# Key, query and value projections ahead of the spatial ones, the linear attention beside 48 weight tiles, the spatial gate inside it in a PSUM bank of its own

## The chip, the cores and the metric

The kernel runs on one core of one Trainium2 chip. The metric is the device time of one execution in microseconds (us); lower is better. TensorE is called PE below, VectorE DVE, ScalarE ACT, GpSimdE POOL, and SyncE SP.

## What is computed

Two transformer blocks in a row, on 256 tokens of width 1024, in fp32. The change touches the token mixer of the second block only. Cut to that:

```python
z = h @ w_in                                   # 8 parts: u vs q r ga gb k v, and lr (32 columns)
u, vs, q, r, ga, gb, k, v, lr = split(z)
vn = layer_norm(gelu(vs), sgu_ln_g, sgu_ln_b)
s  = einsum('gpq,bnqgc->bnpgc', sgu_w, vn) + sgu_b      # spatial gate
a  = gelu(u) * s
la = log_sigmoid(lr @ w2 + b2) / 16            # log decays, two directions
o  = gla_forward(q, k, v, la_f, s0f) + gla_backward(q, k, v, la_b, s0b)   # chunks of 64 tokens
ob = o * rsqrt(mean(o*o) + eps) * gla_norm_g * silu(r)
x  = x + g1 * ((sigmoid(ga) * (a @ w_br_a) + sigmoid(gb) * (ob @ w_br_b)) @ w_o)
```

`s0f` and `s0b`, the initial states, come from the same recurrence over a second input, the context (`ctx`), for which k, v and lr alone are projected. With the mean and variance of the layer norm taken per token, the gain `sgu_ln_g` and the shift `sgu_ln_b` are per column of `vs`.

## The kernel before

Every weight tile ("slot") is 128 x 1024 numbers and comes by its own DMA into one of six raw buffers. ACT rounds it to `w_hi` (`fill` in `act_program`, L776), DVE subtracts to `w_lo` (`fill` in `dve_program`, L1235), both in rings of four, and PE multiplies with three fp32r matmuls for each product: `tall` (L318 to L320, 24 matmuls over 256 tokens, one output chunk of 128 columns) or `wide` (12 matmuls over 512 columns). While PE works on slot s, the slots s+1 to s+3 can be ready; the `fill` of slot s+4 waits until PE has used slot s, since it overwrites its buffer.

The order is written out by hand, and each engine runs its own list strictly in order. For a stage of n slots, ACT does for each slot: evacuate the product (`evac`), `fill` for slot s+4, and one step of a side task; DVE does `fill` for s+4 and one step of its side task; PE does the slot and one step of its side task. A side task is a generator (`Side`), each `yield` of which ends a step. So step k stands behind slot k of the stage on every engine, and behind the fill that waits for PE's slot k on ACT and DVE. `claim(bank)` on PE waits until whoever reads a PSUM bank has released it; the releaser stands in `emptied`.

The product of slot n goes to bank n % 4 (`RING`), banks 0 to 3; the side tasks use banks 4 to 7. `project_tokens` uses banks (0, 1) and then (2, 3) for four slots each.

The stages of the second block's mixer before, with their side tasks:

- `u` (8 slots), `vs0`, `vs1` (4 wide slots each), beside `context_states`: log decays of the context, their scans, the decayed keys (the product with the keys on POOL, L1889), PE transposes, initial states.
- `lr`, `k`, `q`, `v0`, `v1` (17 slots), beside `spatial_gating`: gelu of `vs` and `u`, the norm (its gain and shift on POOL, L1905 and L1907), eight small PE products in four pairs, one pair for each of banks 4 to 7, then bias and gate on DVE (L1552, L1557, L1560).
- `r`, `ga`, `gb`, `br_a` (32 slots), beside `linear_attention`: log decays, scans, decayed keys (POOL), scores, three steps of the state in halves, the outputs (`gla_o`), the head norms (`sum`, `power`), `r_scaled` on POOL, `ob` and `ob_low`.
- `br_b`, `w_o2`, and the feed-forward part.

In `log_decays` before, DVE adds the bias (L1487), takes minus the absolute value (L1493), ACT takes exp and ln (L956, L958), and DVE combines (L1498).

Of the kernel before, what the change touches and what calls it, by code (L numbers as in the profile page):

```python
# [7 lines left out]
P = 128  # L8
D = 1024
# [33 lines left out]
          ("u", KC), ("vs0", 4), ("vs1", 4), ("lr", 1), ("k", 4), ("q", 4), ("v0", 4), ("v1", 4),  # L43
# [26 lines left out]

def raw_of(kind, n):
    return LOAD_OF[kind, n] % RAW
# [10 lines left out]
def down_slot(l, j):  # L83
# [5 lines left out]
             ("gla_b2", 2 * GH), ("gla_g", 8), ("fconv", 9 * FC), ("fconv_b", FC)]  # L89
VEC_AT, VEC_N = {}, 0  # L90
for _name, _n in VEC_PARTS:
# [7 lines left out]
    "decay_act": ("decay_exp", "decay_ln", "kd_exp", "q_exp", "k_exp", "dec"),  # L99
    "conv_act": ("img", "conv_mid", "conv_first"),  # L100
    "gates_act": ("sig_a", "sig_r", "sig_b", "vs_gelu", "u_gelu"),
    "memory_dve": ("ma_max0", "ma_max", "ma_rc", "ma_prob", "ma_lo"),
    "stick_dve": ("z_kept", "minus_log_not", "log_not_first", "log_not", "log_a", "am_part", "am"),
    "decay_dve": ("decay_b", "decay_abs", "decay", "scan", "decay_left"),
# [6 lines left out]
    "spatial_dve": ("sg_bias", "sg_gated", "sg_lo"),  # L111
    "vs_normed": ("vn_scaled", "vn"),
# [4 lines left out]
class Signals:  # L117
# [56 lines left out]
def build(nc, table, stream, vec, xT, memT, ctxT, c_rows, sq_consts, masks, scan_mask, sgu_bc, sgu_wT, gla_w2, out):  # L174
    pe, act, dve, pool, sp = nc.tensor, nc.scalar, nc.vector, nc.gpsimd, nc.sync
    with ExitStack() as ctx:
# [26 lines left out]
        LR = sb("LR", [P, T])  # L203
# [34 lines left out]
        BC, WS = area(20736, 3, D), area(23808, KC, P)  # L238
        UB, VSB = area(0, KC, T), area(2048, TT, D)
        RB, GA, GB = area(4096, KC, T), area(6144, KC, T), area(8192, KC, T)  # L240
        KB, QB, VB = area(10240, GH, T), area(11264, GH, T), area(12288, TT, D)
        QD = area(14336, 2, GH, T)
        KI, KD = area(0, 2, GH, T), area(2048, 2, GH, T)
        CKI, CKD = area(6144, 2, GH, T), area(8192, 2, GH, T)
        ST = [area(at, 2 * GH, 256) for at in (16384, 18432, 0, 10240)]
# [62 lines left out]
        def pe_program():  # L308
# [46 lines left out]
            def project(stage, count, h, release, side=None, ready=None, steps=1):  # L355
                assert n == AT[stage], (stage, n)
                for i in range(count):
                    b = n % RING
# [174 lines left out]
            def log_decays(s):  # L533
                for d in range(2):
                    claim(4 + 2 * d, 5 + 2 * d)
                    pe.wait_ge(*past("lr", s))
                    for hh in range(GH):
                        last = mm(PS[:, 4 + 2 * d + hh // 2, (hh % 2) * T:(hh % 2 + 1) * T],
                                  W2[32 * d:32 * d + RANK, hh * P:(hh + 1) * P],
                                  LR[32 * d:32 * d + RANK, :], hh % 2 == 0, True)  # L540
                    last.then_inc(*mark("decay_z", s, d))
                    emptied[4 + 2 * d] = emptied[5 + 2 * d] = [("decay_b", s, d, GH - 1)]
                    yield
                yield from nothing(4)

            def transpose_kd(s, kd):
                pe.wait_ge(*past("kd", s, 1))
                for d in range(2):
# [26 lines left out]
            def spatial_gating():  # L575
# [3 lines left out]
                for c in range(KC):  # L579
                    b = 4 + c // 2  # L580
                    if c % 2 == 0:
                        claim(b)
# [3 lines left out]
                    if c % 2 == 0:  # L586
                        continue
# [1465 lines left out]
```

## Time and profile before

| | us |
|---|---|
| median of the timed runs (3) | 1255.36 (1255.06 to 1255.45) |
| profiled execution, its own time | 1260.26 |
| its span, first to last instruction | 1258.9 |
| PE busy (matmul) | 1177.7, 94% |
| DVE busy | 846.1, 67% |
| ACT busy | 626.4, 50% |
| POOL busy | 218.8, 17% |
| mean granted clock of PE | 0.975 of full |

PE is busy for nearly the whole span, so what is won or lost is the time in which it stands still or runs at the lower clock. All positions below are us from the start of the span. The stages that the change touches lie between 718.68, PE's first matmul of `u`, and 994.24, its first of `br_b`; `w_o2` starts at 1019.49.

### The profile page before, as it was taken

How to read it: one execution, taken by the hardware profiler on the slowest of the kernel's cores; microseconds unless marked ns; L12 is line 12 of the kernel's file. 1: busy time of each engine (PE TensorE's matmuls, PEld its weight loads, DVE VectorE, ACT ScalarE, POOL GpSimd, SP SyncE). 2: the span in 40 equal slices, each digit the busy share in tenths (PEclk: the TensorE clock that was granted, in tenths of full speed). 3: DMA queues.
4: the chain of work that ended last, by engine and by line, in shares of the span. 5: the costliest groups of instructions: out<-in, count | busy, mean ns of one | idle time of the engine just before them, and what ended most of it. 6: DMA issues, size and time to landing. Idle time of an engine off the chain costs nothing.

```text
span 1258.9 us, 21745 instructions
## 1 busy us (share of the span) xinstructions
PE 1177.7 (94%) x8974; PEld 1132.0 (90%) x8974; DVE 846.1 (67%) x1234; ACT 626.4 (50%) x942; POOL 218.8 (17%) x156
## 2 busy tenths in 40 slices
PE   6999999999889799999999998999799897999996
PEld 5989999999888689999999887889789797999996
DVE  4577677778764656777787664766663576777775
ACT  5645534435555545444446545544721545555553
POOL 2002100001210012000000001300100112565562
PEclk9999999999989799999999999999899898999999
DMA  7545687776543045778876444454342263546540
GB/s 290 171 158 183 192 277 250 242 239 228 198 159 122 12 186 180 247 242 269 268 251 215 157 131 148 138 163 134 118 128 84 75 194 108 181 164 192 190 162 34
DMA packets 60321, 222.91 MB, mean 177 GB/s; under 512 B 6736, under 2 KB 6992, under 8 KB 59584
## 3 DMA queue, kind: packets, MB, share of 16 engines
q1 hardware_dynamic: 59760, 219.05, 53.2%
q10 hardware_dynamic: 288, 2.10, 0.4%
q8 instruction: 71, 1.16, 0.4%
q0 software_dynamic: 176, 0.39, 0.1%
q14 instruction: 26, 0.21, 0.1%
HBM read 220.46 MB, written 1.05 MB: 176 GB/s over the span
## 4 chain that ended last, share of the span: by engine, by line
PE 76%; DVE 12%; ACT 6%; issue 3%; POOL 2%; DMA 1%; SPq 0%; ACTq 0%; DVEq 0%; POOLq 0%
PE PS L318 21%; PE PS L320 21%; PE PS L319 21%; PE PS L323 13%; DVE w_lo L1235 4%; ACT w_hi L776 3%; DMA X<-xT 1%; DVE SQ L1271 1%; DVE ARENA L1755 1%; DVE SQ L1509 1%; ACT ARENA L858 1%; POOL ARENA L1905 1%; DVE ARENA L1271 1%; POOL ARENA L1907 0%; DVE raw L1257 0%
## 5 line engine op out<-in xcount | busy, mean ns | idle before, releaser
L1235 DVE TENSOR_TENSOR w_lo<-raw,w_hi 128x1024 fp32r<-128x1024 f32 x325 | 410.3, 1265 | 276.2 <-ACT w_hi L776 275.7
L776 ACT ACTIVATE w_hi<-raw 128x1024 fp32r<-128x1024 f32 x356 | 372.1, 1053 | 156.3 <-PE PS L320 131.8
L318 PE MATMUL PS<-Y_hi,w_hi 128*128 128x256 f32 x1240 | 360.7, 291 | 20.7 <-DVE Y_lo L1633 5.9
L319 PE MATMUL PS<-Y_lo,w_hi 128*128 128x256 f32 x1240 | 355.0, 286 | 0.0
L320 PE MATMUL PS<-Y_hi,w_lo 128*128 128x256 f32 x1240 | 354.9, 286 | 0.0
L318 PEld LDWEIGHTS PS<-Y_hi,w_hi 128*128 128x128 f32 x1240 | 242.2, 195 | 28.6 <-issue 17.4
L319 PEld LDWEIGHTS PS<-Y_lo,w_hi 128*128 128x128 f32 x1240 | 242.4, 195 | 0.1
L320 PEld LDWEIGHTS PS<-Y_hi,w_lo 128*128 128x128 f32 x1240 | 242.1, 195 | 0.0
L318 PE MATMUL PS<-H_hi,w_hi 128*128 128x256 f32 x808 | 233.1, 288 | 5.5 <-issue 2.5
L319 PE MATMUL PS<-H_lo,w_hi 128*128 128x256 f32 x808 | 229.1, 284 | 0.0
L320 PE MATMUL PS<-H_hi,w_lo 128*128 128x256 f32 x808 | 229.0, 283 | 0.0
L318 PEld LDWEIGHTS PS<-H_hi,w_hi 128*128 128x128 f32 x808 | 155.5, 192 | 10.6 <-issue 5.8
L319 PEld LDWEIGHTS PS<-H_lo,w_hi 128*128 128x128 f32 x808 | 155.6, 193 | 0.2
L320 PEld LDWEIGHTS PS<-H_hi,w_lo 128*128 128x128 f32 x808 | 155.5, 192 | 0.0
L318 PE MATMUL PS<-G_hi,w_hi 128*128 128x256 f32 x528 | 149.6, 283 | 3.4 <-DVE G_lo L1363 3.4
L319 PE MATMUL PS<-G_lo,w_hi 128*128 128x256 f32 x528 | 149.4, 283 | 0.0
L320 PE MATMUL PS<-G_hi,w_lo 128*128 128x256 f32 x528 | 149.4, 283 | 0.0
L318 PEld LDWEIGHTS PS<-G_hi,w_hi 128*128 128x128 f32 x528 | 101.3, 192 | 3.9 <-DVE w_lo L1235 2.0
L320 PEld LDWEIGHTS PS<-G_hi,w_lo 128*128 128x128 f32 x528 | 101.4, 192 | 0.0
L319 PEld LDWEIGHTS PS<-G_lo,w_hi 128*128 128x128 f32 x528 | 101.4, 192 | 0.0
L1845 POOL TENSOR_TENSOR GF<-GF,RS 128x256 f32<-128x256 f32 x44 | 32.6, 742 | 340.5 <-ACT GF L894 340.5
L894 ACT ACTIVATE GF<-GF 128x256 f32<-128x256 f32 x44 | 18.3, 417 | 145.3 <-DVE GF L1374 145.3
(194 smaller groups left out, 1467.7 us busy)
## 6 DMA issues: line engine op xcount, KB each, us to landing
raw<-stream SPq DMA_DIRECT2D x404, 512.0 KB, 4.0
ARENA<-memT SPq DMA_DIRECT2D x2, 1024.0 KB, 6.0
ARENA<-sgu_bc ACTq DMA_DIRECT2D x1, 1536.0 KB, 11.2
X<-xT SPq DMA_DIRECT2D x1, 1024.0 KB, 11.3
ARENA<-c_rows SPq DMA_DIRECT2D x2, 512.0 KB, 6.9
ARENA<-ctxT SPq DMA_DIRECT2D x1, 1024.0 KB, 7.7
outT<-ARENA SPq DMA_DIRECT2D x2, 512.0 KB, 2.6
CROW<-c_rows SPq DMA_DIRECT2D x1, 512.0 KB, 8.7
```

The source lines that it names most:

```text
L318: pe.matmul(o, wh, xh, start=start, stop=False, skip_group_check=True)
L319: pe.matmul(o, wh, xl, start=False, stop=False, skip_group_check=True)
L320: return pe.matmul(o, wl, xh, start=False, stop=stop, skip_group_check=True)
L323: return pe.matmul(o, w, x, start=start, stop=stop, skip_group_check=True)
L776: act.activation(w_hi[n % RING][:], raw[at][:], ACT.Copy).then_inc(*mark("hi", n))
L858: act.activation(EX[:, i], PS[:, bs[h], t * T:(t + 1) * T], ACT.Exp, bias=nmx[:, i:i + 1], scale=HD ** -0.5, accum_out=sm[:, i:i + 1]).the ...
L894: act.activation(GF[:], GF[:], ACT.Silu).then_inc(*mark("silu", l, j))
L1235: dve.tensor_tensor(w_lo[n % RING][:], raw[raw_of("slot", n)][:], w_hi[n % RING][:], ALU.subtract).then_inc(*mark("lo_dve", n))
L1271: dve.scalar_tensor_tensor(via[:, c], src[:, c], g(c), rs[1], ALU.mult, ALU.mult).then_inc(*mark("norm", tag, c))
L1509: dve.tensor_tensor_scan(dst, first, src, 0.0, ALU.mult, ALU.add).then_inc(*mark("scan", s, d, hh))
L1755: dve.scalar_tensor_tensor(ACC[:, b + 1 - k], IMG[:, r0:r0 + ROWS, c0:c0 + COLS], gain("fconv", j + t * FC), ACC[:, b + 1 - k], ALU.mult, ...
L1845: pool.tensor_tensor(GF[:], GF[:], RS[:, 0], ALU.mult).then_inc(*mark("silu_rs", l, j))
```

## The change

The stages are reordered to `lr`, `k`, `q`, `v0`, `v1` (17 slots, beside `context_states`) and then `u`, `vs0`, `vs1`, `r`, `ga`, `gb`, `br_a` (48 slots, beside one `linear_attention`, in which the spatial gate lies). Steps are now named: `pace.to(k)` makes what follows it part of step k. From stage `r` to `w_o2` the slots use three banks (0 to 2), and bank 3 serves the spatial gate and, as before, the head norms. ACT takes the absolute value straight out of PSUM with the bias added, in four instructions for a direction, and DVE's bias instruction takes the minimum with 0 as well. The decayed keys are made by DVE. The gain and shift of the layer norm leave POOL: the gain is applied behind the product, the shift goes into the bias through two more PE products (`sg_rows`) and eight DVE instructions. Three things of the arithmetic have their own buffers now (two of `KB`, two of `VB`, two halves of `LR`). The DMA of `sgu_bc` shrinks from 1536 KB to 512 KB.

The steps of the parts that the diff below leaves out: in both new side tasks, PE has the log decays in steps 1 and 2; ACT has their absolute values, exp and ln in 2 and 3; DVE has the minimum in 2 and 3, `decay` and the scan of one direction in 4 and 5, of the other in 6 and 7, `decay_left` in 8 and 9, the decayed keys in 10 and 11. Beside the context, DVE has the eight `sg_bias` instructions in step 8, and ACT has `kd_exp` in 9 and 10, the copies of the transposes in 13. In `linear_attention`, ACT has `q_exp` and `k_exp` in 6 and 8, `dec` and `kd_exp` in 9 and 10, the copies of the transposes in 14, the gelu of `vs` in 17, that of `u` and the table of exp in 18, the layer norm's root in 19; DVE has `qd` in 12 and 13, `ki` in 14 and 15, the masked copies of the scores (`sc`) in 17, the statistics of `vs` in 18, `silu_r` in 28 to 31, `ob` in 36 to 39 and `ob_low` in 41 to 44.

```diff
@@ order of the stages, and the banks
-          ("u", KC), ("vs0", 4), ("vs1", 4), ("lr", 1), ("k", 4), ("q", 4), ("v0", 4), ("v1", 4),
+          ("lr", 1), ("k", 4), ("q", 4), ("v0", 4), ("v1", 4), ("u", KC), ("vs0", 4), ("vs1", 4),
+def bank_of(n):
+    return n % 3 if AT["r"] <= n < AT["ffn2"] else n % RING
+class Pace:
+    def __init__(self):
+        self.at = 1
+    def to(self, step):
+        while self.at < step:
+            self.at += 1
+            yield
@@ pe_program, context_states
-                yield from log_decays(0)
-                yield from nothing(7)
-                yield from transpose_kd(0, CKD)
+                yield from log_decays(0, pace)
+                yield from pace.to(6)
+                claim(4, 5)
+                pe.wait_ge(*past("late_in", 1))
+                for half in range(2):
+                    last = mm(PS[:, 4 + half].rearrange("p (c q) -> p c q", c=4), ONES, WS[:, 4 * half:4 * half + 4])
+                last.then_inc(*mark("sg_rows"))
+                emptied[4] = emptied[5] = [("sg_bias", KC - 1)]
+                yield from pace.to(12)
+                transpose_kd(0, CKD)
+                yield from pace.to(15)
...
@@ pe_program, the gate
+            def spatial_gating(pace):
+                for c in range(1, KC, 2):
+                    yield from pace.to(21 + c // 2)
+                    claim(3)
+                    pe.wait_ge(*past("vs_unit", 1))
+                    for k in (c - 1, c):
+                        for t in range(TT):
+                            last = mm(PS[:, 3, (k % 2) * T + t * P:(k % 2) * T + (t + 1) * P],
+                                      VSB[:, t, k * P:(k + 1) * P], WS[:, k], k % 2 == 0 and t == 0, True)
                     last.then_inc(*mark("sg", c // 2))
+                    emptied[3] = [("sg_gated", c // 2)]
@@ pe_program, linear_attention
+                yield from pace.to(13)
+                transpose_kd(1, KD)
+                yield from pace.to(16)
                 pe.wait_ge(*past("ki", 1))
...
+                    if step == GN - 2:
+                        yield from spatial_gating(pace)
+                    for turn in range(2 * GH):
+                        if turn % GH == 0:
+                            yield from pace.to((18, 20, 25)[step] + turn // GH)
+                        hh, d = turn // 2, turn % 2
+                        i = d * GH + hh
...
                 for hh in range(GH):
+                    yield from pace.to(28 + hh)
...
                 for hh in range(GH):
+                    if hh % 2 == 0:
+                        yield from pace.to(33 + hh // 2)
                     if hh % 2 == 0:
                         claim(3)
@@ act_program, log_decays; linear_attention
+                    yield from pace.to(2 + d)
+                    act.wait_ge(*past("decay_z", s, d))
+                    for hh in range(GH):
+                        act.activation(tmp[:, d, hh], PS[:, 4 + 2 * d + hh // 2, (hh % 2) * T:(hh % 2 + 1) * T],
+                                       ACT.Abs, bias=gain("gla_b2", d * GH + hh)).then_inc(*mark("decay_abs", s, d, hh))
...
+            def spatial_gating(pace):
                 for c in range(1, KC, 2):
+                    yield from pace.to(22 + c // 2)
                     act.wait_ge(*past("sg_gated", c // 2))
+                    act.activation(Y2[0][:, c - 1:c + 1], UB[:, c - 1:c + 1],
                                    ACT.Copy).then_inc(*mark("sg_hi", c // 2))
+                yield from pace.to(27)
+                act.wait_ge(*past("r", KC - 1))
+                act.activation(GB, RB, ACT.Sigmoid).then_inc(*mark("sig_r"))
+                exp_set()
+                yield from pace.to(32)
                 act.wait_ge(*past("gla_o", GH - 1))
...
                 for i in range(2):
+                    yield from pace.to(34 + i)
                     power(f"head{i}", RS4[:, 2 * i:2 * i + 2], PS[:, 3].rearrange("p (h t) -> p h t", h=2), 1.0 / 256,
                           ("sum", f"head{i}"))
                 for hh in range(GH):
+                    yield from pace.to(41 + hh)
+                    if hh == 0:
+                        act.wait_ge(*past("gb", KC - 1))
+                        act.activation(GA, GA, ACT.Sigmoid).then_inc(*mark("sig_a"))
+                        act.activation(GB, GB, ACT.Sigmoid).then_inc(*mark("sig_b"))
+                        exp_set()
+                    ob_split(hh)
@@ dve_program
+                yield from pace.to(19)
+                states(0, 0)
+                yield from pace.to(20)
+                states(0, 1)
+                vs_units()
+                yield from pace.to(21)
+                states(1, 0)
                 dve.wait_ge(*past("sc", 1))
                 dve.tensor_tensor(SC[:, 0], SC[:, 0], SC[:, 1], ALU.add).then_inc(*mark("sc_sum"))
+                yield from pace.to(22)
+                states(1, 1)
+                yield from spatial_gating(pace)
+                for half in range(2):
+                    yield from pace.to(26 + half)
+                    states(2, half)
@@ dve_program, the gate
+            def spatial_gating(pace):
                 for c in range(1, KC, 2):
+                    yield from pace.to(22 + c // 2)
+                    two = slice(c - 1, c + 1)
                     dve.wait_ge(*past("sg", c // 2))
                     for k in range(2):
+                        v = PS[:, 3, k * T:(k + 1) * T].rearrange("p (t q) -> p t q", t=TT)
+                        dve.scalar_tensor_tensor(v, v, gain("sgu_g", c - 1 + k),
+                                                 SB[:, c - 1 + k].unsqueeze(1).to_broadcast([P, TT, P]), ALU.mult,
+                                                 ALU.add).then_inc(*mark("sg_scaled", c // 2, k))
+                    dve.wait_ge(*past("sg_scaled", c // 2, 1))
                     dve.wait_ge(*past("u_gelu", 1))
+                    dve.tensor_tensor(UB[:, two], PS[:, 3].rearrange("p (c t) -> p c t", c=2), UB[:, two],
                                       ALU.mult).then_inc(*mark("sg_gated", c // 2))
                     dve.wait_ge(*past("sg_hi", c // 2))
+                    dve.tensor_tensor(Y2[1][:, two], UB[:, two], Y2[0][:, two],
                                       ALU.subtract).then_inc(*mark("sg_lo", c // 2))
```

## Rows read from the trace of the kernel before

**Rows 1.** The page, busy time of each engine over the span

```profile
PE 1177.7 (94%) x8974; PEld 1132.0 (90%) x8974; DVE 846.1 (67%) x1234; ACT 626.4 (50%) x942; POOL 218.8 (17%) x156
```

**Rows 2.** Windows, three side tasks, `br_b`: us, PE, PEld, DVE, ACT, POOL busy, PE clock, DMA

```profile
718.68:782.14 63.46, 58.57 (x353) 51.48 (x352) 37.47 (x39) 31.00 (x37) 4.75 (x2) 1.00 0.47 151
782.14:839.59 57.45, 53.81 (x347) 48.80 (x345) 37.90 (x36) 30.52 (x40) 12.53 (x4) 0.97 0.42 138
839.59:946.20 106.61, 99.16 (x712) 93.32 (x712) 70.69 (x89) 51.53 (x69) 4.74 (x2) 0.95 0.41 129
946.20:1019.49 73.29, 67.17 (x537) 65.99 (x537) 36.07 (x56) 28.55 (x34) 5.40 (x4) 0.95 0.32 101
```

**Rows 3.** Windows from slot start to slot start: slots alone, then with side products

```profile
852.53:864.05 11.52, 11.52 (x98) 11.52 (x97) 4.72 (x4) 6.40 (x8) 0.00 (x0) 1.00 0.34 112
750.27:758.43 8.16, 8.16 (x38) 6.76 (x37) 8.16 (x12) 1.06 (x1) 0.00 (x0) 1.00 0.50 170
721.64:726.63 4.99, 4.99 (x34) 4.34 (x33) 3.26 (x6) 1.33 (x2) 0.00 (x0) 1.00 0.57 167
828.34:834.69 6.35, 6.35 (x34) 5.40 (x33) 5.35 (x8) 2.65 (x3) 0.00 (x0) 1.00 0.37 112
898.75:902.50 3.75, 3.75 (x35) 3.75 (x34) 3.75 (x4) 3.53 (x4) 0.00 (x0) 1.00 0.45 144
...
963.85:971.19 7.34, 7.34 (x66) 7.34 (x65) 1.65 (x2) 1.06 (x1) 0.00 (x0) 1.00 0.24 74
772.61:782.14 9.53, 9.53 (x47) 8.25 (x46) 2.45 (x2) 4.44 (x5) 0.00 (x0) 1.00 0.74 249
```

**Rows 4.** Timeline of PE: start, duration, line, and its idle time before, with releaser

```profile
813.91 1.71 PE L323 MATMUL PS<-ARENA 128*128 128x128 f32 x8 [2.01 <-POOL ARENA L1907]
...
839.59 0.39 PE L318 MATMUL PS<-Y_hi,w_hi 128*128 128x256 f32 x1 [1.11 <-ACT ARENA L844]
...
884.40 0.36 PE L318 MATMUL PS<-Y_hi,w_hi 128*128 128x256 f32 x1 [2.73 <-DVE w_lo L1235]
...
890.28 0.55 PE L318 MATMUL PS<-Y_hi,w_hi 128*128 128x256 f32 x1 [2.77 <-DVE w_lo L1235]
...
917.91 1.96 PE L323 MATMUL PS<-ARENA,SQ 64*128 64x256 f32 x8 [1.08 <-DVE ARENA L1595]
...
994.24 0.55 PE L318 MATMUL PS<-Y_hi,w_hi 128*128 128x256 f32 x1 [5.87 <-DVE Y_lo L1633]
```

**Rows 5.** Timeline of ACT behind the slot that ended at 929.34

```profile
929.45 0.38 ACT L833 ACTIVATE ARENA<-PS 128x256 f32<-128x256 f32 x1 [3.65 <-PE PS L320]
929.73 1.05 ACT L776 ACTIVATE w_hi<-raw 128x1024 fp32r<-128x1024 f32 x1
```

**Rows 6.** Timeline of DVE behind the same slot, and in the gate before

```profile
821.77 0.75 DVE L1552 TENSOR_TENSOR SQ<-PS,ARENA 128x256 f32<-128x256 f32 x2
822.55 0.69 DVE L1557 TENSOR_TENSOR SQ<-SQ,ARENA 128x512 f32<-128x512 f32 x1
...
916.45 1.32 DVE L1595 COPY_PREDICATED ARENA<-mask_sb,PS 128x1024 f32<-128x1024 uint32 x1
...
930.81 1.23 DVE L1235 TENSOR_TENSOR w_lo<-raw,w_hi 128x1024 fp32r<-128x1024 f32 x1 [2.19 <-ACT w_hi L776]
931.95 1.65 DVE L1611 SCALAR_TENSOR_TENSOR ARENA<-ARENA,small,PS 128x256 f32<-128x256 f32 x4
```

**Rows 7.** Timeline of ACT in the first head norm, and a table load

```profile
983.82 0.69 ACT L787 ACTIVATE ARENA<-PS,EPS_COL 128x512 f32<-128x512 f32 x1 [1.10 <-PE PS L323]
984.54 0.63 ACT L789 ACTIVATE ARENA<-ARENA 128x512 f32<-128x512 f32 x1
...
997.07 1.28 ACT L1178 ACT_TABLE_LOAD   x1
```

**Rows 8.** Windows behind the wait ahead of `br_b`, and at 890.28

```profile
994.24:998.60 4.36, 4.36 (x19) 4.09 (x20) 3.51 (x6) 2.78 (x4) 1.00 (x1) 0.50 0.02 4
...
890.28:895.54 5.26, 5.26 (x25) 5.26 (x26) 2.70 (x3) 4.97 (x7) 0.00 (x0) 0.50 0.64 199
```

More of the change, by code:

```diff
@@ L110 @@
     "modulation": ("mod_dot", "mod"),
[L111 to L112 removed]
+    "spatial_dve": ("sg_bias", "sg_scaled", "sg_gated", "sg_lo"),
 }
@@ L1510, in scans, with decayed_keys @@
                                                ALU.add).then_inc(*mark("scan", s, d, hh))
-                    yield
+            def decayed_keys(s, d, kd):
+                dve.wait_ge(*past("kd_exp", s, d))
+                dve.wait_ge(*past("kb", s, GH - 1))
+                dve.tensor_tensor(kd[:, d], kd[:, d], KB[s], ALU.mult).then_inc(*mark("kd", s, d))
             def context_states():
+                pace = Pace()
                 dve.wait_ge(*past("norm_hi", "norm1", KC - 1))
-                yield from log_decays(0, CKI)
-                yield from scans(0, CKI, ONES[:, 0:1].to_broadcast([P, T]))
+                yield from log_decays(0, CKI, pace)
+                yield from pace.to(8)
+                dve.wait_ge(*past("sg_rows"))
+                dve.wait_ge(*past("late_in", 1))
+                for c in range(KC):
+                    dve.scalar_tensor_tensor(SB[:, c], PS[:, 4 + c // 4, (c % 4) * P:(c % 4 + 1) * P], gain("sgu_b", c),
+                                             SB[:, c], ALU.mult, ALU.add).then_inc(*mark("sg_bias", c))
                 for d in range(2):
+                    yield from pace.to(8 + d)
                     e = 0 if d else T - 1
@@ L1624, in linear_attention @@
                                       ALU.mult).then_inc(*mark("ob", hh))
-                    if hh:
-                        ob_low(hh - 1)
-                    yield
-                ob_low(GH - 1)
+                for hh in range(GH):
+                    yield from pace.to(41 + hh)
+                    ob_low(hh)
             def ob_low(hh):
@@ L1711, in dve_program @@
             side = Side(linear_attention())
-            beside(16, side)
-            dve.wait_ge(*past("sig_r"))
-            for c in range(KC):
-                dve.scalar_tensor_tensor(RB[:, c], RB[:, c], gain("gla_g", c), GB[:, c], ALU.mult,
-                                         ALU.mult).then_inc(*mark("silu_r", c))
-            beside(KC, side)
+            beside(5 * KC, side)
             def branch_a(i, s):
@@ L1925, in pool_program @@
             side = Side(linear_attention())
-            fills(4 * KC, side)
+            fills(6 * KC, side)
             side.finish()
```

379 lines of the change are left out of this document (138 added, 241 removed).

## The prediction

> **What bounds the kernel now.** I read the page first: PE is busy 1177.7 us of a span of 1258.9 [rows 1], so only time in which PE stands or runs slowly can move, and work that PE gains or loses. Then windows over the stages, set against what PE has to do in them. A tall slot takes 2.88 us (11.52 for four), a wide one 2.72 (8.16 for three). The side products cost, beyond their slots, 2.11 for a log decay (4.99 - 2.88), 0.91 for a pair of gate products (6.35 - 2 x 2.72), 0.87 for eight transposes (3.75 - 2.88), 4.46 for a `gla_o` (7.34 - 2.88), 6.8 for all context states (9.53 - 2.72) [rows 3]. A half step of the state has the four products of a log decay (2.1), a `scores` twice a gate pair (1.8), a head sum is put at 2.0. From 718.68 to 1019.49 PE has 57 tall slots (164.2), 16 wide (43.5), 4 log decays (8.4), 4 sets of transposes (3.5), the context states (6.8), 4 gate pairs (3.6), 2 scores (3.6), 6 halves (12.6), 4 `gla_o` (17.8), 2 sums (4.0): 268.0. The windows add up to 300.8 [rows 2]. So 32.8 us are loss: 6.0, 6.1, 12.5 and 8.3 in the four windows. This is all that the change can win there. The larger waits show whence it comes: the gain and shift of the norm on POOL (2.01, then a slot at the low clock), two late `w_lo` (2.73 and 2.77, ACT having stood in its queue for `decay_left`), the masked scores (1.08), and 5.87 at `br_b` for the last `Y_lo` [rows 4]. Behind the last one PE runs 4.36 us at half the granted clock, 1.2 GHz; behind the pair, 5.26 [rows 8].
>
> **The change, part by part.** The slots, log decays, transposes, states and outputs are the same in number; only order and side steps differ. So I sum what PE loses in the new order and set it against 32.8. An engine's step k stands behind its fill, and that waits for PE's slot k. The delay of this is in the rows: the slot ended at 929.34, ACT evacuated at 929.45 and filled from 929.73, DVE filled from 930.81, and its step began at 931.95: 2.6 us after the slot [rows 5, 6]. That number decides most of what follows.
>
> 1. New PE work, `sg_rows`: two fp32 products of 512 columns. The context states are 16 of 256 columns in 6.8, so 0.43 each, and this is four times that: +1.8 (1.5 to 2.2).
> 2. Turns of banks, where the next slot needs the bank just filled. Behind a pair of wide banks ACT copies for 1.0 us, and PE idles 1.11 and restarts slowly, 1.4 in all [rows 4]; this falls due at `u`. At `v0` a 0.38 copy does it, 0.7. At `vs0` the same copy comes behind `q_exp` and `k_exp`, 1.1 (0.7 to 1.5). The turn at `r` is hidden by the scores, 3.6. Sum 3.2.
> 3. Context keys: DVE makes `kd` of the second direction in step 11, two steps of DVE work ending about 3.6 behind PE's slot 11, while PE asks after 2.72 + 0.87. With the backlog of the scans and of eight `sg_bias`, each between 0.25 and 0.41 (a 256 column one: 1.65 for four [rows 6]), I take 0.7 (0 to 1.7).
> 4. `ki` of step 15: behind the copies of the transposes ACT fills late, DVE's fill and `ki` end 6.8 after slot 14, and PE asks after two wide slots, 5.4: 1.4 (0.5 to 2).
> 5. Scores: DVE copies two masks of 1.2 each from 2.6 after slot 17, ready at 5.1, and PE wants the second bank at 3.3: 1.75. The trace had 1.08 here [rows 4].
> 6. The gate. PE's four pairs stand in steps 21 to 24, all in bank 3, and each claims the bank from DVE's gating of the one before. But DVE does that in steps 22 to 24, behind the fill for the very slot that PE has just ended. So PE's pair in step 23 waits 2.6 for DVE's step to begin, two scalings (0.9; the two bias instructions took 0.75), the product (0.69 [rows 6]), 0.1 for the signal: 4.3. Step 24 the same. In step 22 DVE has first half a step of the state, four instructions for 1.6 [rows 6]: 5.9. Nothing is left for PE in that time: its next slot stands behind the pair in its own queue, and behind PE's wait ACT and DVE get no used buffer. Sum 14.5. Before, four pairs had four banks and never waited for a gate. Bounds: 12.5 if scalings from PSUM to PSUM are as quick as the bias and restarts are free, 16 if they take 0.2 more.
> 7. The last half of the state stands in DVE's step 27 and PE wants it after slot 28, with no side product between: 2.6 + 1.6 + 0.1 - 2.88 = 1.5.
> 8. Squares of the output: ACT's evacuation comes first now, 0.5.
> 9. Head norms: PE's second sum (step 34) claims bank 3 from ACT's first `power`, moved to step 34 as well: evacuation and fill 1.4, then 0.69 and 0.63 [rows 7]: 2.85. Before, it was in the step of the sum, and hidden.
> 10. `sig_a` and `sig_b` stand together on ACT in step 41: two table loads of 1.28 [rows 7] and two sigmoids of 2048 columns at 1.9 (a fill of 1024 takes 1.05 [rows 5]), 6.3 us; `ob_hi` follows, DVE waits for it ahead of the evacuation of the second `br_a`, and the third slot from there wants its bank of three: 0.8. The 5.87 at `br_b` is gone, since `ob_low` ends four slots ahead.
> 11. Clock. After 5.87 of standing PE ran 4.36 at 1.2 GHz [rows 8], 2.2 lost. Three waits of 4 to 6 us with 3.8 of work between: 2.0 each (1.2 to 2.7), 6.0. For the smaller waits around the scores and head norms 1.5 (0 to 4).
> 12. First tiles of wide stages, 0.3.
>
> The decay chain that cost ga its two waits I put at nothing: its scans are now two steps apart, ACT waits for each alone, about 2 us by the 2.6 above, and three ready slots of weights, 8.6 us, cover that; without this cover it costs up to the old 2.73 + 2.77 and their clock, 8. POOL's products on DVE take a `w_lo`'s 1.23 each [rows 6], which fits beside the fill into a slot's 2.88. The shorter DMA is put at nothing: PE waits for a DMA only at the very start.
>
> Sum: 1.8 + 3.2 + 0.7 + 1.4 + 1.75 + 14.5 + 1.5 + 0.5 + 2.85 + 0.8 + 7.5 + 0.3 = 36.8 against 32.8, +4.0. On the profiled 1260.26 (span 1258.9 and 1.4 around it) this is 1264.3. That execution is 4.9 above the median of the runs; taken over to it: 1255.36 + 4.0 = 1259.4.
>
> **The rivals.** *A, the clock hardly falls.* The first of the two waits for `w_lo`, 2.73, left the clock alone: PE's next matmul took 0.36, the one behind the second 0.55 [rows 4]. If the gates cost 1.2 each and the smaller waits nothing, the sum is 3.9 less: 1255.5, no change. Against it: each gate's wait is over 4 us.
>
> *B, the gates are free.* This holds if DVE gates before PE asks, that is if its step is not bound to the slot, or if the 2.6 are shorter than the pair. Then items 6 and the 6.0 of clock fall away: 1238.9, faster. For it speaks only that the gate before never stood; but it had four banks and two slots to each pair. It decides at a chain of under about 1 us behind the slot, and the rows have 4.3.
>
> *C, the clock stays down.* Once it is low, the three slots, three pairs and the half step behind them run at 1.2 GHz throughout: 8.6 + 2.7 + 2.1 = 13.4 instead of 6.0, which gives 1266.8. The rows for it: the low clock outlasted a whole slot at 890.28 [rows 8], after two waits of 2.7 with a single slot between, the very pattern of the gates. The Trainium skill (TensorE: Matmul & The Clock Gate, A second HAM failure mode: psum-queue depth-cycling) speaks against the change here: a kernel whose matmul groups take turns in PSUM banks pauses so often between them that the clock keeps falling and rising. By that rule C would be the case; the trace agrees for two waits, not beyond.
>
> *D, the old chain comes back.* DVE has the decayed keys, the eight `sg_bias` and the minimum now; if its backlog reaches 6 us in one of the decay chains, `w_lo` is late again, up to 8 more. It would land in C's place, near 1266.
>
> **How the numbers follow.** The forecast has 0.60, A 0.13, B 0.10, C and D together 0.17. The forecast's own range, with the bounds above taken by half, is 1256 to 1262.5. For 8 in 10, A and most of C come in: 1253.5 to 1266. This kernel's measurement tells 0.2% (2.5 us) from no change, so same is 1252.9 to 1257.9. Faster: B and a little of A, 0.12. Same: most of A and the lower edge of the forecast, 0.25. Slower: 0.63.
>
> **What would show it.** PE rows of the gate (four products of 128 columns, bank 3) behind idle times of nearly 5.9, 4.3, 4.3, released by DVE's gating, and a granted clock of a half around them; an idle time of 2.8 ahead of the second head sum, released by ACT's exp; none of more than 1 ahead of `br_b`; the two 2.7 waits for `w_lo` gone; POOL idle from the first block to the head norms. If the waits ahead of the gate are under 1 us, item 6 is wrong and with it the forecast. If they stand but the time is lower, the clock or an item of 2 to 5 is over-priced.

## The result, and the profile after

| | before | after |
|---|---|---|
| median of the timed runs (5 each, taken together) | 1255.45 (1255.06 to 1256.67) | 1263.15 (1261.01 to 1264.79) |
| profiled execution, its own time | 1260.26 | 1264.79 |
| its span | 1258.9 | 1263.5 |
| mean granted clock | 0.975 | 0.974 |

The ratio after to before is 1.0044, 95% interval 1.0033 to 1.0055: on 1255.4 that is 5.5 us slower (4.1 to 6.9). The two medians are 7.7 apart, the two profiled executions 4.5. The five runs after spread over 3.8 us, the 29 runs of the kernel before that were timed beside e1 to e4 over 7.6, and the times go with the granted clock: of the five runs after, the two at 0.979 took 1261, the three at 0.974 to 0.976 took 1263 to 1265. So below, single waits are compared in the traces and totals in the medians. One run of e4, of 1640.72 us at a granted clock of 0.648, is left out of everything below.

The page after, busy time of each engine, answers to [rows 1]:

```profile
PE 1178.6 (93%) x8978; PEld 1132.7 (90%) x8978; DVE 840.2 (66%) x1242; ACT 632.4 (50%) x958; POOL 195.4 (15%) x148
```

Windows of the kernel after, in the columns of [rows 2]: the context's side task; `linear_attention` up to and with the scores; from there up to and with the first gate pair; the slots and pairs of the gate; the rest to `w_o2`; and what follows:

```profile
718.75:783.94 65.19, 62.98 (x382) 55.29 (x380) 36.88 (x47) 34.80 (x47) 0.00 (x0) 1.00 0.45 147
783.94:841.12 57.18, 54.91 (x353) 49.26 (x353) 41.08 (x44) 37.09 (x50) 0.00 (x0) 1.00 0.46 147
841.12:864.30 23.18, 21.36 (x164) 18.83 (x162) 15.41 (x23) 13.38 (x18) 0.00 (x0) 1.00 0.35 115
864.30:901.00 36.70, 22.54 (x125) 21.79 (x123) 14.84 (x25) 5.87 (x9) 0.00 (x0) 0.72 0.18 58
901.00:1021.72 120.72, 115.53 (x937) 113.05 (x937) 63.14 (x89) 56.55 (x72) 7.04 (x4) 0.99 0.41 131
1021.72:1263.50 241.78, 224.45 (x1796) 221.43 (x1794) 173.42 (x283) 126.57 (x208) 115.42 (x60) 0.97 0.45 149
```

The stretch of the last one in the kernel before:

```profile
1019.49:1258.90 239.41, 222.11 (x1796) 219.37 (x1794) 168.68 (x283) 126.55 (x208) 118.40 (x60) 0.98 0.46 150
```

The stages of the change now take 302.97 us, from 718.75 to 1021.72, where they took 300.81. The fourth window is the change's own: 36.70 us, of which PE works 22.5, at a mean clock of 0.72. None of the other four up to `w_o2` has a clock below 0.99. The waits of PE in these stages (us in total, times, the longest), without two smaller ones of 0.5 and 0.3; all together are 25.8:

```profile
PE PS L339 <- DVE ARENA L1572: 14.2, 3, 5.8
PE PS L339 <- ACT ARENA L808: 2.7, 1, 2.7
PE PS L339 <- ACT ARENA L852: 1.9, 2, 1.3
PE PS L339 <- DVE ARENA L1621: 1.5, 2, 1.0
PE PS L339 <- DVE ARENA L1586: 1.5, 1, 1.5
PE PS L334 <- ACT ARENA L863: 1.1, 1, 1.1
PE PS L339 <- DVE ARENA L1614: 0.9, 1, 0.9
PE PS L334 <- DVE ARENA L1741: 0.6, 1, 0.6
PE PS L567 <- DVE ARENA L1519: 0.6, 1, 0.6
```

L1572 is the gate's product on DVE, L808 the exp of a head norm, L852 and L863 the copies out of the banks, L1621 the masked scores, L1586 the states, L1614 `ki`, L1741 the evacuation of `br_a`, L1519 the decayed keys. The old waits for `w_lo` and the 5.87 for `Y_lo` [rows 4] are gone; which part of the change took each away, no run tests. PE's timeline at the gate (start, duration, idle time before, releaser), and DVE's behind the slot in between:

```profile
873.18 2.08 PE L339 MATMUL PS<-ARENA 128*128 128x128 f32 x8 [5.76 <-DVE ARENA L1572]
884.14 2.08 PE L339 MATMUL PS<-ARENA 128*128 128x128 f32 x8 [4.20 <-DVE ARENA L1572]
894.77 2.08 PE L339 MATMUL PS<-ARENA 128*128 128x128 f32 x8 [4.20 <-DVE ARENA L1572]
```

```profile
868.81 1.22 DVE L1244 TENSOR_TENSOR w_lo<-raw,w_hi 128x1024 fp32r<-128x1024 f32 x1 [1.46 <-ACT w_hi L795]
869.95 1.65 DVE L1586 SCALAR_TENSOR_TENSOR ARENA<-ARENA,small,PS 128x256 f32<-128x256 f32 x4
871.52 0.88 DVE L1567 SCALAR_TENSOR_TENSOR PS<-PS,V,ARENA 128x256 f32<-128x256 f32 x2
872.43 0.69 DVE L1572 TENSOR_TENSOR ARENA<-PS,ARENA 128x512 f32<-128x512 f32 x1
...
881.34 1.23 DVE L1244 TENSOR_TENSOR w_lo<-raw,w_hi 128x1024 fp32r<-128x1024 f32 x1 [6.83 <-ACT w_hi L795]
882.48 0.88 DVE L1567 SCALAR_TENSOR_TENSOR PS<-PS,V,ARENA 128x256 f32<-128x256 f32 x2
883.39 0.69 DVE L1572 TENSOR_TENSOR ARENA<-PS,ARENA 128x512 f32<-128x512 f32 x1
```

The granted clock behind the first of these waits, over the pair and over 3.47 us of the slot behind it (us, PE busy, clock, DMA share, GB/s, as in all windows of PE alone below):

```profile
873.18:874.91 1.73, 1.73 (x9) 0.50 0.00 0
874.91:878.38 3.47, 3.47 (x18) 0.50 0.00 0
```

The chain can be read off row by row: the slot ends, ACT and DVE fill, DVE's step begins (half a state first, in one case), two scalings, the product, and only then PE starts its pair. DVE, whom all wait for, stands 6.83 itself, for a fill that waits for PE.

### The profile page after: what moved, and what is told of

The parts are those of the page before. It is cut to its first block, busy times and chain, and to the rows that moved or that the text cites. A ratio compares the mean times of both kernels' runs of the same rounds, so it can differ in the third digit from the quotient of the medians.

```text
span 1263.5 us, 21778 instructions
## 1 busy us (share of the span) xinstructions
PE 1178.6 (93%) x8978; PEld 1132.7 (90%) x8978; DVE 840.2 (66%) x1242; ACT 632.4 (50%) x958; POOL 195.4 (15%) x148
## 4 chain that ended last, share of the span: by engine, by line
PE 78%; DVE 11%; ACT 6%; issue 4%; DMA 1%; SPq 0%; POOL 0%; ACTq 0%; DVEq 0%
PE PS L334 22%; PE PS L335 21%; PE PS L336 21%; PE PS L339 14%; DVE w_lo L1244 3%; ACT w_hi L795 3%; DVE ARENA L1774 1%; DMA X<-xT 1%; DVE SQ L1280 1%; ACT ARENA L877 1%; DVE ARENA L1280 1%; DVE raw L1266 0%; DVE ARENA L1586 0%; PE PS L428 0%; DVE ARENA L1427 0%
## 5 line engine op out<-in xcount | busy, mean ns | idle before, releaser
L1244 DVE TENSOR_TENSOR w_lo<-raw,w_hi 128x1024 fp32r<-128x1024 f32 x325 | 405.6, 1249 | 316.1 <-ACT w_hi L795 315.6
L852 ACT ACTIVATE ARENA<-PS 128x256 f32<-128x256 f32 x70 | 26.7, 382 | 120.1 <-PE PS L336 119.9
```

Source lines behind the costliest of these rows:

```text
L852: act.activation(dst[:, i], PS[:, bank_of(s), 0:T], ACT.Copy).then_inc(*mark(name, *index, i))
L1244: dve.tensor_tensor(w_lo[n % RING][:], raw[raw_of("slot", n)][:], w_hi[n % RING][:], ALU.subtract).then_inc(*mark("lo_dve", n))
```

## The experiments

None of them changes what is computed. They were timed in later rounds than the kernel after, each set beside runs of the kernel before, whose median was 1256.12 for e1 to e4, 1256.84 for e5 to e8 and 1258.10 for e9 and e10, where it had been 1255.45. So a difference of two medians holds up to 2.7 us of drift between rounds. The table therefore has, beside the medians, the difference of the two ratios to the kernel before, taken times 1255.4 ("by ratios"); its error is 2 to 3 us. Since the scatter of the clock reaches into the totals, a second measure is used, taken in each profile: the distance from PE's `sg_rows` to its norm sum behind `w_o2`, which frames all that differs between these kernels. In the kernel after, the two rows are:

```profile
740.24 1.88 PE L339 MATMUL PS<-ARENA,consts 128*128 128x512 f32 x4
...
1046.84 0.67 PE L339 MATMUL PS<-SQ,consts 128*128 128x256 f32 x2 [1.92 <-POOL SQ L1849]
```

This is 306.60 us. The table has the same distance for the others, read from the same two rows.

| kernel | median (runs) | ratio to before, 95% | against after, by ratios | distance | against after, distance |
|---|---|---|---|---|---|
| after | 1263.15 (5) | 1.0044, 1.0033 to 1.0055 | | 306.60 | |
| e1 gate spaced | 1255.16 (12) | 0.9992, 0.9980 to 1.0005 | -6.5 | 298.42 | -8.2 |
| e2 order in the half step | 1261.59 (6) | 1.0049, 1.0036 to 1.0063 | +0.6 | 303.85 | -2.8 |
| e3 PE kept busy | 1256.22 (12) | 1.0009, 0.9992 to 1.0026 | -4.4 | 297.59 | -9.0 |
| e4 head norm's step | 1256.44 (11) | 1.0010, 0.9999 to 1.0020 | -4.3 | 299.21 | -7.4 |
| e5 one direction | 1269.92 (6) | 1.0099, 1.0080 to 1.0119 | +6.9 | 314.19 | +7.6 |
| e6 gate in the same step | 1248.64 (6) | 0.9934, 0.9914 to 0.9954 | -13.8 | 294.14 | -12.5 |
| e7 banks exchanged | 1261.07 (9) | 1.0031, 1.0021 to 1.0042 | -1.6 | 303.80 | -2.8 |
| e8 combined | 1230.54 (4) | 0.9796, 0.9779 to 0.9813 | -31.1 | 273.49 | -33.1 |
| e9 before, directions mixed | 1254.96 (12) | 0.9978, 0.9967 to 0.9990 | | | |
| e10 combined, outputs later | 1227.08 (4) | 0.9751, 0.9734 to 0.9767 | -36.8 | 271.05 | -35.6 |

### e1: two slots to each gate pair

```diff
-                    yield from pace.to(21 + c // 2)        # PE
+                    yield from pace.to(21 + 2 * (c // 2))
-                    yield from pace.to(22 + c // 2)        # ACT, DVE
+                    yield from pace.to(22 + 2 * (c // 2))
```

and what follows the gate, three steps later. With it, ACT's sigmoid of `r` comes ahead of its last part of the gate, and DVE's last half states stand among its steps for `silu_r`.

> The changed kernel with PE's four gate pairs in steps 21, 23, 25, 27 and the gating of DVE and ACT in 22, 24, 26, 28, still in bank 3 alone; the last state, the outputs and the head norms move back by three steps. Theory G (the gate's claim of bank 3 is bound to DVE's step of the same number): the three idle times of 5.8, 4.2, 4.2 ahead of the gate vanish, and with them some 8 us of half clock; 1241, 22 us under the changed kernel. Rival R (sharing one bank is itself the loss, or the time comes back later): the waits shrink but others grow; less than 8 us are won.

```profile
873.01 1.16 PE L339 MATMUL PS<-ARENA 128*128 128x128 f32 x8 [2.89 <-DVE ARENA L1573]
881.24 1.16 PE L339 MATMUL PS<-ARENA 128*128 128x128 f32 x8 [1.32 <-DVE ARENA L1573]
889.47 1.16 PE L339 MATMUL PS<-ARENA 128*128 128x128 f32 x8 [1.32 <-DVE ARENA L1573]
...
908.47 7.78 PE L339 MATMUL PS<-ARENA 128*128 128x128 f32 x39 [3.82 <-DVE ARENA L1587]
```

The waits are not gone, they are 2.87 and 2.88 shorter: exactly one slot. The expectation had them gone altogether. But DVE still gates in the step behind PE's pair, that step is itself bound to a slot's end, and the spacing only gives PE a second slot to work on meanwhile. And a new wait of 3.82 stands ahead of the outputs, where the last half states now come behind a fill that came late and behind `silu_r`. At the gate itself the clock stays full (1.00 from 864.12 to 893.43), as the theory had it. But behind the 3.82 it falls: the first output and the slot after it take 12.16 us at a clock of 0.58, where they take 7.41 in the kernel after. So 1255.2 and not 1241: 8.0 us are won by the medians, 6.5 by the ratios, the size that rival R gave. The miss says that distance alone, by one slot, is the poorer remedy.

### e6: the gate's DVE part in PE's own step

```diff
-                    yield from pace.to(22 + c // 2)        # ACT, DVE
+                    yield from pace.to(21 + c // 2)
```

and the half states of steps 21 and 22 behind the gates.

> The changed kernel with DVE's and ACT's part of each gate in the very step of PE's pair (21 to 24 instead of 22 to 25), the state halves of step 1 behind the gates; the pairs stay in consecutive steps and in the one bank 3. Theory S (the gate waits come from the step in which DVE stands, one slot behind PE's pair, and not from the bank being one): the chain behind a slot is 2.6 + 0.9 + 0.7 + 0.1 = 4.3, and PE asks after the pair and the next slot, 3.8: waits of 0.5, growing to at most 2 as the two state halves (1.6 each) are put on DVE between the gates; 14.2 of waits become 2 to 4 and most of the 7 us of clock goes too: 1243 to 1249. Rival B (one bank for four pairs costs its 4 us whatever the step): waits and time stay, 1263. Rival W (DVE's added load in these steps makes a w_lo late): gate waits small, but a wait for w_lo of 2 to 4 around step 24 to 26, 1250 to 1254.

```profile
869.52 1.05 PE L339 MATMUL PS<-ARENA 128*128 128x128 f32 x8
875.26 1.61 PE L339 MATMUL PS<-ARENA 128*128 128x128 f32 x8 [1.82 <-DVE ARENA L1572]
880.87 1.16 PE L339 MATMUL PS<-ARENA 128*128 128x128 f32 x8
```

The pairs are as close together as after, and all in bank 3; still 12.4 of the 14.2 are gone, and the time is 14.5 us less by the medians, 13.8 by the ratios. From the first pair to the half step behind the last slot, 37.55 us became 19.14. This is theory S: with the same single bank, 1.8 of waiting is left, and in e8 none. What costs is that DVE's answer stands one step behind PE's question, so that DVE begins it only when PE, its slot done, already asks for the bank again. The clock gained nothing on balance in this profile: the 6.0 us won at the gate beyond the waits were lost in two stretches at half clock elsewhere, 3.0 and 3.2; the windows from the scores' wait on, ahead of all that the edit touches, and in the outputs:

```profile
848.55:855.71 7.16, 7.16 (x31) 0.53 0.23 76
...
897.49:908.06 10.57, 10.57 (x64) 0.68 0.24 84
```

### e3: the same waits, PE kept busy in them

```diff
...
                     yield from pace.to(21 + c // 2)
+                    if c > 1:
+                        busy_work(36 if c == 3 else 24)   # products into the next slot's bank, overwritten by it
                     claim(3)
...
```

`busy_work` itself claims that bank and waits for the next slot's weights first.

> The changed kernel with idle work on PE ahead of the second, third and fourth claim of the gate: 36, 24 and 24 extra products of the next slot's weights (results are overwritten), about 4.3, 2.9 and 2.9 us, which end before the bank comes free. Theory C (about 8 of the gate's 22 us are the half clock behind its waits): the clock stays at full, the slots behind take 2.9 to 3.1 again, 8 us faster, 1255. Rival (the clock costs nothing beyond the waits): within 1 us of the changed kernel.

Idle times of 1.45, 1.32 and 1.32 are left, and the window over the gate has PE at full clock throughout:

```profile
864.39:893.68 29.29, 25.19 (x207) 1.00 0.22 72
```

In the kernel after, the same stretch:

```profile
864.30:900.96 36.66, 22.50 (x123) 0.72 0.18 58
```

36.66 less 29.29 is 7.4, with the chains of DVE unchanged: that is what the low clock costs at the gate, on top of 14.2 of standing. The distance fell by 9.0, as one more stretch of low clock is missing: the second head sum waits 2.66, as after, but it and the slot behind it then take 4.70 us at a clock of 1.00, against 6.36 at 0.73. Useless work on PE brings 6.9 us by the medians, 4.4 by the ratios, and two of the twelve runs, at 1263.25 and 1264.37, gained nothing. So the clock's part at the gate is shown in the trace; how much of it reaches the total is known only to 2 or 3 us.

### e4: the head norm's power in the step of its sum

```diff
-                    yield from pace.to(34 + i)
+                    yield from pace.to(33 + i)
                     power(f"head{i}", RS4[:, 2 * i:2 * i + 2], ...
```

> The changed kernel with ACT's roots of the head norms in steps 33 and 34 instead of 34 and 35. Theory H: the idle 2.65 us ahead of the second head sum goes, and with it a stretch of half clock that falls due behind it; 2.7 to 4 us faster, 1259.5 to 1260.5. Rival: ACT then waits for the sum ahead of its next fill and a slot comes late; no gain.

```profile
943.23 1.96 PE L339 MATMUL PS<-SQ,consts 128*128 128x256 f32 x8 [0.46 <-ACT SQ L1054]
947.90 1.89 PE L339 MATMUL PS<-SQ,consts 128*128 128x256 f32 x8
```

The 2.65 are gone. The distance fell by 7.4, more than the edit can give. In the kernel after, the slot ahead of the second sum (with the wait), the sum itself and the slot behind it took 3.0, 1.4 and 0.5 more than they must, the last two at a clock that had fallen; 4.6 of this is gone. The median is 6.7 lower, 4.3 by the ratios. The other 2.8 fell in the gate, which the edit does not touch (see e2).

### e2: another order within the half step

```diff
-                        hh, d = turn // 2, turn % 2
+                        hh, d = 2 * (turn // GH) + turn % 2, turn // 2 % 2
```

> The changed kernel with the four state products of a half step in the order of one direction after the other, so that neighbours lie on the same 64 rows of PE more often; in the changed kernel they alternate. Theory K (alternating halves of the array run at the same time, which halved them from 1.92 to 1.07 us): each of the six blocks goes back to about 1.9 or, with one boundary left, 1.7, and the kernel is 4 to 5 us slower, 1267.5. Rival (the shorter blocks have another cause, such as the banks): no change in the blocks, 1263.

The half steps take what they took, 1.07 for the most part, so the order within one does not matter, and by the ratios the time is that of the kernel after (0.6 us apart). The trace shows why: the products of the second direction, third and fourth in the program, start 0.014 us behind those of the first, and the signals of the two directions come 0.013 apart, at the end of the half step. The 2.8 us by which the distance is shorter are not its doing: the waits of the gate are the same 5.76, 4.20 and 4.20, but the stretches at half clock fall otherwise over them. The same window as above:

```profile
861.68:895.55 33.87, 19.71 (x123) 0.80 0.19 62
```

33.87 for what took 36.66. So one and the same part of the program, with the same waits, takes 2.8 us more or less by where and how long the clock is low: by the mean clocks of the two windows, an estimate, 13.5 us at half clock here and 20.5 after.

### e5: one direction to a half step

```diff
-                        hh, d = turn // 2, turn % 2
+                        hh, d = turn % GH, turn // GH
```

and DVE's states likewise.

> The changed kernel with each half step of the state made of one direction again, as in the kernel before: its four products then lie on the same 64 rows, where the changed kernel has two on rows 0 to 63 and two on rows 64 to 127, whichever way they are ordered. DVE's states follow the same order. Nothing else differs. Theory K (products on opposite row halves run at the same time, two by two, and this is the 5 us by which the change does less PE work than I summed): the records of a half step start one by one, 0.22 us apart, not in pairs; each of the six half steps costs 1.9 instead of 1.07, and the time is 1267 to 1268.5 (1263.15 + 5). Rival (the halves are cheap for another cause, their place in the order or their banks): the records still start in pairs, the time stays 1263.

PE's rows for a half step, first this kernel, then the one after (eight records, for four products):

```profile
902.02 1.99 PE L339 MATMUL PS<-ARENA,SQ 64*128 64x256 f32 x8
907.00 1.99 PE L339 MATMUL PS<-ARENA,SQ 64*128 64x256 f32 x8
```

```profile
900.96 1.14 PE L339 MATMUL PS<-ARENA,SQ 64*128 64x256 f32 x8
905.10 1.13 PE L339 MATMUL PS<-ARENA,SQ 64*128 64x256 f32 x8
```

Start by start in the trace, the records begin one by one here, 0.22 apart; after and in e2 they begin two by two, 0.006 to 0.014 apart, and the next two 0.22 later. From the start of a half step to its slot it is 1.92 against 1.07. It is not a matter of banks: in e2 the four products go two by two into two banks, as they do here, and are paired. So theory K holds: a product over rows 0 to 63 and one over rows 64 to 127 run at the same time. In the kernel before, a half step had only the one or the other; the new turn order mixes them. The time is 6.8 us up by the medians. The blocks take 5.1 more (6 times 0.85), but PE, coming later, no longer waits for the second masked copy of the scores (0.48, and a slow restart) nor for the norm ahead of the gate (0.3): from the first half step to the first gate pair's end it is 17.79 here and 16.17 after, 1.6 more for four half steps. So 1.8 of the 5.1 are saved again as waits and restarts, and 3.3 are the net price. The other 4.7 of the distance are clock: the first output and the slot behind it take 12.13 at 0.58, where they take 7.41 after; the gate takes 0.4 less.

### e9: this part of the change alone, in the kernel before

```diff
-                    for i in range(2 * GH):
-                        hh, d = i % GH, i // GH
+                    for turn in range(2 * GH):
+                        hh, d = turn // 2, turn % 2
+                        i = d * GH + hh
```

and DVE's states in the order 0, 1, 4, 5, 2, 3, 6, 7.

> The kernel before with one part of the change alone: each half step of the state takes two products of either direction, in turn, and DVE's states follow in that order. Nothing else is moved. Theory K (the pairs on opposite row halves run together in any kernel): the records of a half step start two by two, six half steps lose 0.85 each, 1255.4 - 5 = 1250.4. Rival (it needs the new order around it): the records stay one by one, 1255.4. Rival P (PE is faster but what follows waits more, the weights of DVE or the next state): pairs in the trace, but new waits of about the same sum, 1253 to 1255.

```profile
917.86 0.67 PE L323 MATMUL PS<-ARENA,SQ 64*128 64x256 f32 x2 [1.09 <-DVE ARENA L1595]
920.07 2.06 PE L323 MATMUL PS<-ARENA,SQ 64*128 64x256 f32 x6 [1.54 <-DVE ARENA L1595]
927.26 1.13 PE L323 MATMUL PS<-ARENA,SQ 64*128 64x256 f32 x8
```

Five of six half steps shrink to 1.07 here too. The first does not: it now wants a bank of the second masked copy of the scores already, and waits 1.54 more for it, with 7.19 us at a clock of 0.53 from there on. From the first half step to `br_b` the two profiles differ by only 1.1 us (75.26 and 76.33). The median is 1254.96 beside 1258.1 for the kernel before in the same rounds, 0.22% less (0.10 to 0.33%): 2.8 us (1.3 to 4.1), between theory K and rival P; the pairing is theory K's, the new wait rival P's.

### e7: banks exchanged at the wide stages

```diff
-            project_tokens("v0", 512, H2, (0, 1), ("vb", 1, 0), side)
-            project_tokens("v1", 512, H2, (2, 3), ("vb", 1, 1), side)
+            project_tokens("v0", 512, H2, (2, 3), ("vb", 1, 0), side)
+            project_tokens("v1", 512, H2, (0, 1), ("vb", 1, 1), side)
```

and the same for `vs0` and `vs1`, on PE and ACT.

> The changed kernel with the two bank pairs of v0 and v1 exchanged, and those of vs0 and vs1: the stage takes first the banks that its predecessor did not fill last. No other edit. Theory: the waits ahead of v0 (0.52), u (1.11) and vs0 (1.33) go, with the slower products behind them; time 1263.15 - 3.0 = 1260.2. Rival (ACT's late copies are then waited for one slot on, at u's third slot or r's second): waits of the same size one or two slots later, time 1263.

In the waits of this kernel the rows of L852 and L863 are missing, which stood for 1.9 and 1.1 after, and one has grown from 0.6:

```profile
PE PS L567 <- DVE ARENA L1519: 1.2, 1, 1.2
```

PE comes earlier to the decayed keys and waits for them longer. The gain is 2.8 us in the distance, 2.1 by the medians and 1.6 by the ratios, near the expected 3.0 less this 0.6.

### e8 and e10: all of it together

e8 has the gate pairs in steps 21, 23, 25 and 27 on PE, DVE and ACT alike, the last state step in 27 and 28, the outputs from 31, the scores in 17, the head norms as e4, the banks as e7. ACT's and DVE's other steps move with them, as in e1.

> The changed kernel with all that its waits point to: gate pairs in steps 21, 23, 25, 27 on PE, DVE and ACT alike; last state step in 27 and 28 and the outputs from 31; scores in step 17 instead of 16; each head norm's power in the step of its sum; the exchanged banks of e7. The same computation. Theory: the chain of 4.3 behind a slot is shorter than the 6.7 to the next pair, so no gate waits; gone are 14.2 of gate waits, 1.5 ahead of the outputs, 2.7 at the head norm, 3.0 at the banks, 0.9 at ki, about 1 at the scores, and 8 to 10 of clock: 1263.15 - 32 = 1231 (1227 to 1238). Rival (the backlog of DVE and ACT comes out elsewhere, as the 3.82 ahead of the outputs when the gates were only spaced): a single new wait of 3 to 4 with its clock, 1238 to 1243.

```profile
870.17 1.05 PE L339 MATMUL PS<-ARENA 128*128 128x128 f32 x8
876.81 1.05 PE L339 MATMUL PS<-ARENA 128*128 128x128 f32 x8
...
894.14 4.65 PE L339 MATMUL PS<-ARENA 128*128 128x128 f32 x40 [2.26 <-DVE ARENA L1593]
```

The window from the scores to the end of the mixer:

```profile
836.12:1010.00 173.88, 171.15 (x1409) 1.00 0.43 141
```

No gate waits. In this window PE is busy for 171.15 of 173.88 us, at full clock. One wait of more than 0.5 is left in it, 2.26 ahead of the outputs. e10 starts them one step later:

> The combined version of e8 with the outputs and all behind them one step later (outputs from 32, sums 37 and 38, the product with the gate from 40, its low parts from 44). In e8 the outputs waited 2.26 for the last half state, as ACT's sigmoid and its tables had held up the fills. Theory: the wait is gone, nothing new comes up: 1230.54 - 2.3 = 1228.2. Rival: the wait moves with the step, as DVE's backlog does not shrink over one slot, or the low parts of the last product now come late for br_b: 1230.5 or more.

```profile
893.71 4.57 PE L339 MATMUL PS<-ARENA 128*128 128x128 f32 x40
```

```profile
836.12:1006.00 169.88, 169.41 (x1396) 1.00 0.45 144
```

The first is PE's row of the outputs, with no idle time, the second the window as above. 1227.08 is 2.5% below the kernel before and 36 us below the changed one. So the order of stages that the change brings need not lose; what cost was where some side steps stood in it. Whether the old order, with its side steps placed as carefully, would be as fast, no run tests.

## Why the prediction was right, point by point

The forecast was slower by 4.0 us, with a range of 1253.5 to 1266. Measured are 5.5 (4.1 to 6.9) by the ratio and 1263.15 as median. The direction, the gate as its cause and the range held; the median lies 0.65 above the narrower range of the forecast's own case, 1256 to 1262.5. That the sum came near is luck: it came out through two errors against each other, which the slot starts in the trace show, and half of the loss in the profiles arose where the sum does not reach. Each term below is the time beyond a slot's 2.88 or 2.72 and the price of its side product, restarts included:

| term | forecast | measured |
|---|---|---|
| `sg_rows` | 1.8 | 1.7 |
| bank turns v0, u, vs0 | 0.7, 1.4, 1.1 | 0.8, 1.3, 1.6 |
| decayed keys of the context | 0.7 | 0.9 |
| `ki` | 1.4 | 1.1 |
| scores | 1.75 | 2.3 |
| gate, standing | 5.9 + 4.3 + 4.3 | 5.76 + 4.20 + 4.20 |
| gate, clock | 6.0 | 7.9 |
| last half state | 1.5 | 1.6 |
| squares | 0.5 | 0.6 |
| head norm, and the clock of the smaller waits | 2.85 + 1.5 | 4.7 |
| `br_a` | 0.8 | 0.9 |
| others | 0.3 | 0.6 |
| half steps of the state | 0 | -5.0 |

- **The gate** was right in mechanism and in size. The chain of 2.6 behind a slot, taken from other steps [rows 5, 6], carried over to 0.1. e6 and e3 take it apart: without the lag of one step 12.4 of the 14.2 go, with PE kept busy the clock's part goes (7.4 in the trace). Rival B (gates free) fell: its condition, a chain of under 1 us behind the slot, was not met.
- **The clock** was under-sized. I took 2.0 for each of three waits; the measured 7.9 is 2.6 each, still inside my 1.2 to 2.7. The clock was low for the pair and most of the slot behind each wait, and full again before the next wait began. Rival C, that it stays down throughout the gate, did not come true, and its price of 13.4 was not reached; rival A, that it hardly falls, was wrong for waits over 4 us. The waits of 2.89 and 1.32 at e1's gate did leave the clock full. The Trainium skill (TensorE: Matmul & The Clock Gate, A second HAM failure mode: psum-queue depth-cycling) tells of a kernel that takes turns in PSUM banks and whose clock falls and rises between groups of matmuls. The trace agrees in kind, with 0.72 over the gate. But falling and rising is what the forecast had, so I was wrong to count that rule for C.
- **The head norm** was right as a wait (2.65 for 2.85), but the sum behind it and the next slot ran slowly as well.
- **The step that failed**, though the forecast as a whole held, is the first sentence of the part by part: "The slots, log decays, transposes, states and outputs are the same in number; only order and side steps differ. So I sum what PE loses". The number was the same, the price was not. The diff showed the new turn order, and I read it as order alone. It takes 5.0 off PE (six times 1.92 to 1.07, little more in some). e5 gives that back, e9 shows it in the kernel before. Part of it was not won: PE comes earlier to the masked scores and waits there, which is part of why that term is 2.3 and not 1.75, and net of such waits the mixing is worth 3.3 (e5).
- **The balance.** At `w_o2` the changed kernel was 2.2 behind the kernel before, in the two profiles, not 4.0: some 3.3 more of loss, 5.0 less of work, and `sg_rows` 0.1 less. The other 2.3 of the 4.5 arose behind `w_o2`, in the feed-forward part, which the change does not touch. PE does the same 1796 matmuls there in 222.11 us before and 224.45 after, at a clock of 0.98 and 0.97, so these 2.3 are clock and not waits. Why the clock was lower there stays open; with runs of one kernel 4 us and more apart, it may be scatter.
- **The decay chain** (rival D) did not come back: no wait for `w_lo` is left in these stages.

## What to carry to other kernels

When a side product moves into a bank of its own with a second engine emptying it, write down for each turn in which step the emptying engine stands and what binds that step. If it is bound to the slot that PE just ended, each turn costs that engine's whole way (here 2.6 plus its work), less the work that PE has between that slot and its next question: none in the kernel after, one slot in e1, which took off 2.88, a pair and a slot in e6, which took off nearly all. Putting the answer into the step of the question was worth 12.5 us of the distance, spreading the questions 8.2. And where only an order changes, the price of each block must be read again: a new order may let products run together that did not before.

## What the runs showed of the hardware

- Two fp32 products over 64 rows each run at the same time when one lies on rows 0 to 63 and the other on rows 64 to 127: four of 256 columns took 1.07 us mixed (1.34 and 1.46 in two of the six half steps) and 1.92 on one half, in both kernels (after and e5, e9 and before), and in either order within the four (A B A B after, A A B B in e2). In e2 a product thus started ahead of one that stands before it in the program, on the other half of the rows.
- A stretch at half clock after a wait is not tied to the wait's length alone: in e8 a wait of 2.26 left the clock full, in e6 the scores' waits of 1.01 and 0.48 were followed by 7.16 us at a clock of 0.53, and the same two waits in the kernel after left it full (1.00 in the third window); the 2.65 at the head norm was followed by 6.36 us at 0.73 after, the 2.66 in e3 by 4.70 at 1.00. Identical waits of 5.76, 4.20 and 4.20 cost 2.8 us more or less from one program to the next (36.66 and 33.87 for the same stretch). The five runs of the kernel after spread over 3.8 us, so a single profile can't tell apart totals that differ by less.
- Removing waits over the whole mixer brought more than their sum: 33.1 less distance in e8, of which 21.8 are waits of PE (25.8 in the mixer of the kernel after, 4.0 left in e8's), the rest clock and restarts.
